# Products of the condition with later stages' modulation weights, formed on GpSimd by two instructions in place of one on VectorE

## The reference, cut to what matters

```
mod = silu(c) @ w + b                      # w is 1024 x 3072, float32
shift, scale, gate = split(mod, 3)
h = rmsnorm(x, norm_w) * (1 + scale) + shift
x = x + gate * stage(h)
```

## Time and profile before

| | |
|---|---|
| median of three runs | 2639.32 us (2631.01 to 2642.67) |
| span of the profiled execution | 2637.7 us |
| TensorE busy | 2425.0 us, 92% |
| VectorE busy | 1984.6 us, 75% |
| ScalarE busy | 1431.5 us, 54% |
| GpSimd busy | 210.9 us, 8% |

### The profile page before, as it was taken

How to read it: one execution, slowest core, us unless ns; L and a number is a source line. 1 busy time by engine, 2 the same in 40 slices (tenths; PEclk the granted TensorE clock), 3 DMA queues, 4 the chain that set the end, 5 groups by cost and what they waited for, 6 DMA issues and landing times.

```text
span 2637.7 us, 32879 instructions
## 1 busy us (share of the span) xinstructions
PE 2425.0 (92%) x13850; PEld 2105.0 (80%) x13850; DVE 1984.6 (75%) x2208; ACT 1431.5 (54%) x1594; POOL 210.9 (8%) x265
## 2 busy tenths in 40 slices
PE   4877899898899999999999999998997999897998
PEld 3756799687777888888888888887886997886997
DVE  6756777686657888989888889886666775767675
ACT  3312443464546777767676767675444653444562
POOL 1101001000000000000000000000311110221110
PEclk8986899897889999999999999999998999998999
DMA  9652678432246999999999999995224453323551
GB/s 317 214 201 88 213 273 297 161 133 92 96 171 231 348 361 347 360 349 359 352 354 345 360 342 365 340 368 186 96 76 151 162 211 136 115 78 118 197 185 76
DMA packets 263559, 608.44 MB, mean 231 GB/s; under 512 B 18472, under 2 KB 33083, under 8 KB 263403
## 3 DMA queue, kind: packets, MB, share of 16 engines
q1 hardware_dynamic: 247808, 554.39, 58.4%
q0 software_dynamic: 14640, 51.49, 5.7%
q10 hardware_dynamic: 954, 0.37, 0.1%
HBM read 605.17 MB, written 1.05 MB: 230 GB/s over the span
## 4 chain that ended last, share of the span: by engine, by line
PE 80%; DVE 10%; ACT 5%; DMA 2%; issue 1%; POOL 1%; SPq 0%; PEldq 0%; PEld 0%; DVEq 0%; ACTq 0%; POOLq 0%
PE ps L132 78%; PE ps L136 2%; DVE eb L153 1%; DMA slots<-in_hyb_mod_w 1%; DVE X L153 1%; ACT L142 1%; DVE ul_in L145 1%; DVE xn L153 1%; DVE macc L153 1%; ACT uh_ffn L139 0%; DMA beside<-in_dense_mod_w 0%; ACT eb L139 0%; ACT xn L139 0%; DVE ul_ssm_w L145 0%; DVE gate L153 0%
## 5 line engine op out<-in xcount | busy, mean ns | idle before, releaser
L145 DVE TENSOR_TENSOR ul_moe_w<-slots,uh_moe_w 128x2048 fp32r<-128x2048 f32 x334 | 762.6, 2290 | 108.4 <-ACT uh_moe_w L139 108.2
L139 ACT ACTIVATE uh_moe_w<-slots 128x2048 fp32r<-128x2048 f32 x334 | 640.1, 1918 | 215.7 <-PE ps L132 188.9
L132 PE MATMUL ps<-uh_moe_w,XGh 128*128 128x512 f32 x896 | 356.6, 398 | 3.1 <-DVE XGl L145 2.1
L132 PE MATMUL ps<-uh_moe_w,XGl 128*128 128x512 f32 x896 | 349.5, 390 | 0.0
L132 PE MATMUL ps<-ul_moe_w,XGh 128*128 128x512 f32 x896 | 348.9, 389 | 0.0
L145 DVE TENSOR_TENSOR ul_ffn<-slots,uh_ffn 128x2048 fp32r<-128x2048 f32 x62 | 142.1, 2292 | 100.7 <-ACT uh_ffn L139 100.7
L132 PE MATMUL ps<-HTf,uh_ffn 128*128 128x256 f32 x704 | 201.2, 286 | 2.8 <-DVE HTlf L145 2.8
L132 PE MATMUL ps<-HTf,ul_ffn 128*128 128x256 f32 x704 | 200.8, 285 | 0.0
L132 PE MATMUL ps<-HTlf,uh_ffn 128*128 128x256 f32 x704 | 200.8, 285 | 0.0
L132 PEld LDWEIGHTS ps<-uh_moe_w,XGh 128*128 128x128 f32 x896 | 168.3, 188 | 38.8 <-DVE XGl L145 2.3
L132 PEld LDWEIGHTS ps<-uh_moe_w,XGl 128*128 128x128 f32 x896 | 168.2, 188 | 35.8
(11 more groups left out here) (511 smaller groups left out, 5565.0 us busy)
## 6 DMA issues: line engine op xcount, KB each, us to landing
slots<-in_moe_w_gu SPq DMA_DIRECT2D x111, 2048.0 KB, 8.6
slots<-in_moe_w_down SPq DMA_DIRECT2D x56, 2048.0 KB, 8.1
slots<-in_w_up SPq DMA_DIRECT2D x20, 2048.0 KB, 7.9
slots<-in_w_in SPq DMA_DIRECT2D x14, 2048.0 KB, 8.5
slots<-in_dense_w_gu SPq DMA_DIRECT2D x10, 2048.0 KB, 10.1
slots<-in_ssm_w_in SPq DMA_DIRECT2D x10, 2048.0 KB, 8.1
slots<-in_w_down SPq DMA_DIRECT2D x10, 2048.0 KB, 8.4
slots<-in_dense_w_down SPq DMA_DIRECT2D x5, 2048.0 KB, 12.3
```

The source lines that it names most:

```text
L132: return self.e.matmul(o, lhsT, rhs, start=start, stop=stop, skip_group_check=skip) if self.e else DONE
L139: return self.e.activation(o, i, f, **kw) if self.e else DONE
L145: return self.e.tensor_tensor(o, a, b, op) if self.e else DONE
```

## The change

GpSimd forms the products. The first chunk of a part is one multiplication into `macc`, as before. For each of the other seven, GpSimd multiplies the chunk by its column of `sc` in the chunk's own buffer, waits for that to be complete, and adds the buffer to `macc`. VectorE keeps only the work on the sums (`column_done` and the gate additions). TensorE's sums wait for GpSimd's semaphore in place of VectorE's, and `last`, the wait for TensorE before `macc` is overwritten, moves from VectorE's queue into GpSimd's.

```diff
     def side_gpsimd(e, me):
 
         free = [S.t.at(("cols", now[-1])), NOTHING, S.t.at(("mod", "hyb", 1))]
+        last = NOTHING
         ...
                 if n + 2 < len(chunks):
                     get(n + 2)
                 yield
-                free[n % 3] = side.v.at((name, n))
+                e.wait_ge(*S.v.at("sc"))
+                e.wait_ge(*beside_landed[n % 3].at((name, n)))
+                if k == 0:
+                    e.wait_ge(*last)
+                    e.tensor_scalar(macc[:, :], bufs[n % 3], sc[:, 0:1], ALU.mult).then_inc(*side.g.up((name, n)))
+                else:
+                    e.tensor_scalar(bufs[n % 3], bufs[n % 3], sc[:, k:k + 1], ALU.mult).then_inc(*side.g.up())
+                    e.wait_ge(*side.g.now())
+                    e.tensor_tensor(macc[:, :], bufs[n % 3], macc[:, :], ALU.add).then_inc(*side.g.up((name, n)))
+                free[n % 3] = side.g.at((name, n))
                 if k == KC - 1:
+                    last = side.t.at(("gate", name, 1) if part == 2 else ("mod", name, part))
         ...
     def side_vector(e, me):
-        last = NOTHING
         ...
                 yield
-                e.wait_ge(*beside_landed[n % 3].at((name, n)))
-                if k == 0:
-                    e.wait_ge(*last)
-                    e.tensor_scalar(macc[:, :], bufs[n % 3], sc[:, 0:1], ALU.mult).then_inc(*side.v.up((name, n)))
-                else:
-                    e.wait_ge(*side.v.at((name, n - 1)))
-                    e.scalar_tensor_tensor(macc[:, :], bufs[n % 3], sc[:, k:k + 1], macc[:, :], ALU.mult, ALU.add).then_inc(*side.v.up((name, n)))
         ...
     def side_tensor(e, me):
         ...
-                    column_sums(e, side.t, macc, side.v.at((name, n)), name, part, c.side_banks)
+                    column_sums(e, side.t, macc, side.g.at((name, n)), name, part, c.side_banks)
         ...
-                    e.wait_ge(*side.v.at((name, n)))
+                    e.wait_ge(*side.g.at((name, n)))
```

More of the change, by code:

```diff
@@ L989, in side_vector @@
                     column_done(e, side.t, side.v, name, part)
-                    last = side.t.at(("mod", name, part))
                     me.done.add((name, ("cols", part)))
@@ L999, in side_vector @@
                     c.psum.leave(("gate", name, i), side.v)
-                last = side.t.at(("gate", name, 1))
                 me.done.add((name, "rows"))
```

## The result

| | before | after |
|---|---|---|
| median of four runs | 2640.99 us (2631.01 to 2643.08) | 2760.20 us (2759.19 to 2760.56) |
| span of the profiled execution | 2637.7 us | 2758.5 us |
| TensorE busy | 2425.0 us | 2445.3 us |
| VectorE busy | 1984.6 us | 1955.3 us |
| GpSimd busy | 210.9 us | 661.2 us |

The ratio is 1.0467, 95% interval 1.0445 to 1.0489: 119 us slower. The forecast was 2692, with a range of 2642 to 2740: the direction came, the size did not.

The account below looks back on a forecast made before the run. TensorE, 80% of the chain, was taken as the bound, with VectorE's latencies on the chain in the attention part. Terms -13 + 14 + 12 + 38 + 2 = +53 us gave 2692 us, range 2642 to 2740.

Parts of the forecast that it names:

- The multiplication: GpSimd's multiplication of a 128x1024 chunk: 1.3 us, between a memset's 1.0 and the addition's 2.4.
- third rival: Multiplication as dear as the addition, 2.4 us; five dense-stage loops and one hybrid loop late: +47, 2737 us; chance 0.15.
- The rest of the chunk: Per chunk on GpSimd: DMA issue 0.53 us, addition 2.44, gaps of 0.1; TensorE's sum per loop 1.84 us.
- VectorE's cost to GpSimd: Dense stage: GpSimd waits 0.8 of VectorE's 90 us; five parts take 247 us against 209, +38 us at moe's gate.
- GpSimd's cost to VectorE: Dense stage: 67 VectorE operations wait 0.85 us each, 57 us, not felt by TensorE.
- the sign of 2.9: Expected in the changed profile: VectorE's `ul_dense_w` group with a mean above 2.9 us.
- Relief: VectorE loses its fused operations and multiplications, 97 us; worth -13 us in the hybrid stage, 0 in the dense stage.
- Between dense's part 0 and ssm's: Hybrid stage: two-input VectorE operations on the chain wait for GpSimd, +12 us; GpSimd's other loops fit, costing nothing.
- Part 0: Dense's part 0 in the hybrid stage: ready 27 + 14 us after the gate's last sum, stalling TensorE, +14 us.
- Clock: TensorE stalls at dense's part 0 and in the dense stage risk stretches at half clock: +2 us.
- Behind the dense stage: After moe's gate: nothing gives the loss back, since the ssm stage's start waits for that gate; time to the end unchanged.
- The fourth rival: VectorE loses every meeting, waits 163 us in the dense stage and becomes the bound: 2710 us; chance 0.08.

Follow-up runs that it names:

- 1.5 us: Changed kernel, GpSimd multiplying only the first 512 columns of each chunk, by constant 1.0, additions over all 1024: 2703.34 us, ratio 1.0245 to the kernel before.
- neither: Changed kernel without GpSimd's multiplication and addition of the seven later chunks of each part, chunks still loaded: 2623.85 us, ratio 0.9948 to the kernel before.
- memsets: Changed kernel with six GpSimd memsets of about the same total length replacing each later chunk's multiplication and addition: 2700.27 us, ratio 1.0242 to the kernel before.
- spread column: Changed kernel, full computation, the seven later multiplications as tensor_tensor with the column of sc spread over the columns: 2761.59 us, ratio 1.0458 to the kernel before.

## Why the prediction was right in direction and too low

How late TensorE's sums are against the earlier trace rows, by the forecast, in the changed kernel, and in the run with a multiplication of 1.5 us:

| | forecast | after | 1.5 us |
|---|---|---|---|
| dense's part 0 (128.51 before) | +14 | +24 | +13 |
| ssm's part 0 (285.07) | +13 | +40 | +21 |
| mean loop of the dense stage | 49 us | 59.1 | 49.3 |
| moe's gate (493.92) | +51 | +126 | +59 |
| whole | +53 | +121 (spans) | +64 (spans) |

The same profiles cut at these sums, with those of three experiments, in us:

| stretch | before | neither | memsets | after | 1.5 us | spread column |
|---|---|---|---|---|---|---|
| start to dense's part 0 | 128.5 | 125.1 | 147.7 | 152.8 | 141.9 | 155.9 |
| to ssm's part 0 | 156.6 | 149.5 | 159.6 | 172.0 | 164.3 | 177.8 |
| to moe's gate (five loops) | 208.9 | 208.2 | 244.0 | 295.5 | 246.5 | 274.2 |
| to the end | 2143.8 | 2133.0 | 2148.2 | 2138.3 | 2149.5 | 2153.4 |

The forecast missed by 68 us: 49 of them lie in the dense stage, 16 between dense's part 0 and ssm's, 10 at dense's part 0, and the rest of the kernel and the clock's 2 us take 7 back.

- **The multiplication** is the step that failed. I took 1.3 us, near the memset, and held the addition's 2.4 to be the upper bound because a second input could only add. It takes 2.84, above the bound, which is 8 x 1.54 = 12.3 us in each loop. My third rival had the right mechanism with 2.4 us; its sum, 2692 + 47, is 2739 (I wrote 2737), and at 2.84 its own working, 6 x 8 x 0.44 more, gives 2760. The kernel with 1.5 us takes 2703, so 57 us hang on this one operation. They hang on its kind as well as on its length: with the spread column, 1.91 us, the kernel takes 2762.
- **The rest of the chunk**: the gap behind an addition, before a DMA issue, is 0.30 us (I had 0.1), the issue 0.60 (0.53). In a part of eight chunks that is 2 us. A sum behind a stall takes 3.6 us, not 1.84. Together 4 us a loop that I did not have.
- **VectorE's cost to GpSimd**: a loop undisturbed is 47 + 3.6 us, so of 59.1 some 9 were spent waiting for VectorE; in the 1.5 us run, 37 + 3 of 49.3, again 9. What the means of GpSimd's groups in the dense stage lie above their undisturbed lengths sums to 44 and 46 us, which is the same. I had 14 (0.8 x 90 us over five loops). This error and the one before nearly cancel, which is why that run falls on the forecast: its agreement is in part luck and does not prove each term.
- **GpSimd's cost to VectorE** in the dense stage: 67 waits of 0.85 us were priced. The 33 subtractions were held 0.43 us on the mean and the 22 of `hTl` 0.75, and the `ul_dense_w` mean came out at 2.72 us, under the sign of 2.9 that I had set.
- **Relief**, -13: measured -13.7; in the profiles 11 us of it stand before moe's gate, 10 of them in the hybrid stage, where I had put them.
- **Between dense's part 0 and ssm's** I had +12 for meetings on VectorE's chain, and nothing for GpSimd's length ("the other loops of the hybrid stage fit"). The stretch is 22 us longer than in the run with neither operation. The memsets, which read nothing, make it 10 us longer by themselves; this is the term that I put at nothing. The other 12 are the meetings, as priced.
- **Part 0**: the stall is 21.7 us for 14, by the longer chunks; 12.6 in the 1.5 us run.
- **Clock**, +2: TensorE's busy time grew by 20.3 us, 18 of them in the dense stage, whose granted clock was 0.83 for 0.97. Only what TensorE does while GpSimd waits for it lengthens a loop, and that is the sum, counted above.
- **Behind the dense stage** nothing is given back by design, as forecast. The stretch from moe's gate to the end is 2138 us for 2144; the ssm stage's first 175 us had a granted clock of 0.91 for 0.85. Over the profiles here this stretch ranges from 2130 us (clock 0.92) to 2153 (0.82), so differences of 10 us between two kernels can arise in it.
- **The fourth rival**, VectorE as the bound, held in none of the changed kernels; with the spread column VectorE is busy 193 us of the dense stage's 274, for 137 of 295 in the changed kernel.

Account: leaving out both operations gives -14 us against the kernel before, the memsets +76 against that, and the changed kernel +60 against the memsets. That these add up to the loss is no check, since each is a step from one run to the next; what they tell is the share of each cause. By stretches the last step is +5, +12, +51 and -10 us: in each of the five loops 9 us of waits for VectorE and nearly 2 of the chunk's length, which the memsets fell short of. Why one input meets VectorE less than two stays open. No run gave the side work a second accumulator, so what GpSimd's own waits for TensorE's sums (36.7 us in all) cost is not shown.

## What to carry to other kernels

Before an operation goes to an engine on which the trace has no example of it, its duration decides more than all reasoning on waits. A bound for it must be a row of the same kind of operation, and "fewer inputs, so not dearer" is none. Work moved off a busy engine is free only while the new engine's loop, with its issue gaps and the waits that each engine puts on the other, fits the shortest distance between two uses of the result. An experiment that changes data must be read with the counts of data-dependent work beside it.

## What the runs showed of the hardware that was not expected

- GpSimd multiplies 128x1024 by one number to a partition in 2.84 us, by a constant in 2.77, by itself or by a spread column in 1.89, and adds two tensors in 2.34.
- Where both engines have work ready, one operation of VectorE ran between two of GpSimd's at one place (10.40 us for three), and ten of VectorE's ran ahead of one of GpSimd's at another (8.63 us for one).
- VectorE operations with one SBUF input are held too: the chunk's multiplication, 0.75 us alone, took 1.24 on the mean beside additions. Small ones can be held even by memsets. `cu<-cu`, 128x8, took 0.17 us before; these are its two in the changed kernel and in the run of memsets:

```profile
L150 DVE TENSOR_SCALAR cu<-cu x2: 705/711/717, 271.7 to 275.5; 128x8 f32<-128x8 f32 x2
```

```profile
L150 DVE TENSOR_SCALAR cu<-cu x2: 714/856/999, 259.3 to 264.7; 128x8 f32<-128x8 f32 x2
```

The first of each pair runs beside the multiplication of a part's first chunk, and takes 0.71 us in the run with neither operation too. The second is the one that differs: beside memsets it takes 1.00 us, with neither operation 0.17.
